# Feed-forward layers: the row panel of step i-1 moved from behind the up panel of step i to between the gate and the up panel

## The chip, the cores and the metric

The program runs on one core of a Trainium2 chip, as one launch. The metric is the time that the device takes for it, in microseconds. Five engines work side by side, each with its own queue in order: TensorE (PE, with its weight loads shown as PEld), VectorE (DVE), ScalarE (ACT), GpSimd (POOL) and SyncE (SP), which issues the transfers. They wait for each other by semaphores.

## What is computed

The reference is a stack of two blocks over 256 tokens of width 1024, in float32. The change touches only the feed-forward layers of the first block. There are four: `ffn1` and `ffn2` in each of two layers, each with a residual sum of one half.

```python
def swiglu(h, w_gate, w_up, w_down):
    return (jax.nn.silu(h @ w_gate) * (h @ w_up)) @ w_down
...
x = x + 0.5 * swiglu(rmsnorm(x, norm_ffn1[layer]), ffn1_gate[layer], ffn1_up[layer], ...)
```

`w_gate` and `w_up` are 1024 x 2816, `w_down` is 2816 x 1024. Around them stand the mixers (a linear recurrence, a gated delta rule, a gated recurrence) and a second block (retention, dilated attention, a feed-forward part with a squared relu, a gate), which the change leaves as they are.

## The kernel before, in words

**Precision.** Each float32 product is made of three products of a shorter format. A weight panel lands in `raw` (three slots, 1 MB each). ScalarE rounds it to `w_hi` (`split_hi`, L1470), VectorE subtracts to get `w_lo` (`split_lo`, L1947); both have two slots. The activation is split the same way: `u_both` holds the high and low halves of the normed input. An operand for the down product is split to `op_hi` (ScalarE, L1698) and `op_lo` (VectorE, L2015), in four slots.

**Panels.** A panel is one megabyte of weights. A feed-forward layer has 2816 / 256 = 11 steps, numbered 0 to 10. Step i has a **gate panel** and an **up panel** (column panels: all 1024 rows of 256 columns, result in the PSUM banks `colb`), and the down product has a **row panel** for each step: 256 rows of all 1024 columns, added up over the steps in the PSUM tile `acc`. From step 2 on a column panel writes two banks: the high weights meet both halves of the input in one matmul of 512 columns, 16 of them, and then the low weights meet the high half, 16 of 256 columns. A row panel has three thirds in this order: `w_hi` with `op_hi`, `w_lo` with `op_hi`, `w_hi` with `op_lo` (`row_part`, which waits for `w_lo_ready` ahead of the second third and for `op_ready` ahead of the last). The last row panel of a layer waits for all of it at its start.

**Behind a column panel.** ScalarE copies the second bank (`copy_half`, L1515), VectorE adds the first (`add_halves`, L1961). Behind a gate panel ScalarE then takes the silu (L1555). Behind an up panel VectorE multiplies the two into `hid` (L1995), which is the operand of this step: `op_hi` is made from it, and then `op_lo`.

**What sets the order.** `ffn` writes one list, `schedule`, of panels and steps. Every engine walks through the same list and does its part of each entry. With panel p, ScalarE first splits `w_hi` as far as panel p+1 (`split_hi_to`), and VectorE `w_lo` as far as panel p+1 (`split_lo_to`), before they turn to what panel p left in its banks. `split_hi` of panel p waits until TensorE is done with panel p-2, since there are two slots. SP issues the transfer of panel p when both halves of panel p-3 are made. So an entry that changes its place in the list changes it in every queue.

**Other entries.** In layer 0 of `ffn1`, small tables for the mixer are made on VectorE and ScalarE in steps 3 and 4, behind the gate panel (`setup`, `setup_rest`). Row panels 0 to 8 (`by_token`) are summed with tokens in the rows of `acc`. Behind row panel 8 `acc_out` copies `acc` out, and ahead of row panel 9 `acc_turn` (L1062) brings it back transposed with 16 matmuls. Step 0 and the first gate panel work on an input that isn't normed yet.

Of the kernel before, what the change touches and what calls it, by code (L numbers as in the profile page):

```python
# [23 lines left out]
KD = D // P  # L24
DEPTH = 2
D_FF = 2816
PC = 256
# [87 lines left out]
def build(nc, ap, out, stop_at=None):  # L115
    ctx = ExitStack()
    with ctx:
        def sb(name, shape, dt=F32):
            return ctx.enter_context(nc.sbuf_tensor(name, shape, dt))
# [20 lines left out]
        hid = sb("hid", [P, 2, 2 * T])  # L140
# [131 lines left out]
        schedule, panels, ops = [], [], []  # L272
# [8 lines left out]
        def panel(src, kt, ncols, kind, xop, ready, **more):  # L281
            nonlocal n_col, n_act, n_dve, n_row
            r = dict(p=len(panels), src=src, kt=kt, nc=ncols, kind=kind, xop=xop, ready=ready, **more)
            if kind != "row" and early[0]:
                n_scaled[0] += 1
                r.update(xop=g_op(early[1]["ops"]), ready=[], gained=count["fill"] if early[0] == EARLY else None, scaled=n_scaled[0],
                         norm=count["norm"], fill=early[1], half=EARLY - early[0])
                early[0] -= 1
                fresh[0] = True
            elif kind != "row":  # L290
                r["fresh"], fresh[0] = fresh[0], False
            if kind != "row":
                r["c"] = n_col
                n_col += 1
                if r["by"] == "act":
                    n_act += 1
                    r["n"] = n_act
                else:
                    n_dve += 1
                    r["n"] = n_dve  # L300
                bank_users.append((r["by"], r["n"]))
            else:
                n_row += 1
            panels.append(r)
            schedule.append(("panel", r))
            return r
# [33 lines left out]
        def step(name, **more):  # L340
            schedule.append((name, dict(panel=len(panels), nx=count["x"], op=len(ops), **more)))

        def g_op(n_ops):
            def get(kk):
                return tuple(gained_chunk(t, n_ops, kk // 2)[:, kk % 2, :] for t in (op_hi, op_lo))
            return get
# [16 lines left out]
        def pre_norm(gain, at):  # L363


            step("gained", gain=gain, at=at, n=count["fill"] + 1)
            n = norm_sum("x", "fill", gain=gain, at=at)
            f = fill(norm=n, gain=gain, at=at)
            return f

        def x_update(kind, **more):
            count["x"] += 1
            step("x_update", kind=kind, group=count["group"], first=0, **more)
            if kind in ("half", "whole"):
                acc_reader[0] = ("x_updated", 4 * count["x"])
            if kind == "post":
                count["normed"] += 1
                acc_reader[0] = ("acc_normed", 4 * count["normed"])

        def operand(src, ready):  # L380

            r = dict(r=len(ops), src=src, ready=ready)
            ops.append(r)
            return r
# [7 lines left out]
        def kpn(w):  # L392
            return w.rearrange("(k p) n -> p k n", p=P)

        def row_gemm_panel(w, i, r, first, last, base=None, woven=False, by_token=False):
            if r is not None:
                ready = [("op_ready", r["r"] + 1)]
                r["panel"] = len(panels)
                get = op_tiles(r)
            else:  # L400
                ready = base[0]
                get = (lambda kk, i=i: base[1](2 * i + kk))
            if first and acc_reader[0]:
                ready = ready + [acc_reader[0]]
            p = panel(kpn(w)[:, 2 * i:2 * i + 2, :], 2, D, "row", get, ready, first=first, last=last, woven=woven, by_token=by_token)
            if last:
                count["group"] += 1
            return p

        def acc_out():  # L410
            count["turn"] += 1
            step("acc_out", n=count["turn"])
# [3 lines left out]
        def two_banks(r, c0, pair):  # L416


            a = 0 if (c0 % 3 == 0) == (pair == 0) else 2
            r.update(both=n_both[0], banks=slice(a, a + 2),  # L420
                     free=[n for n in range(c0 - 3, c0) if n % 3 in (a, a + 1)] if r["c"] - c0 < 2 else None)
            n_both[0] += 1
            last_both[r["c"]] = n_both[0]

        def ffn(layer, gain, gate, up, down):
            f = pre_norm(gain, KD * layer)
            n = D_FF // PC
            todo = None
            first_both = None
            for i in range(n):  # L430
                g = panel(kpn(gate)[:, :, i * PC:(i + 1) * PC], KD, PC, "A", u_op, [("u_ready", 4 * f)],
                          by="act", evac=("silu_h", len(ops)))
                if i == 2:
                    first_both = g["c"]
                if i >= 2:
                    two_banks(g, first_both, 0)
                if (layer, i, gain) == (0, 3, "norm_ffn1"):
                    step("setup")
                if (layer, i, gain) == (0, 4, "norm_ffn1"):
                    step("setup_rest")  # L440
                if i:
                    step("op_lo", r=todo)
                u = panel(kpn(up)[:, :, i * PC:(i + 1) * PC], KD, PC, "A", u_op, [], by="dve",
                          evac=("h", len(ops), g["n"]))
                if i >= 2:
                    two_banks(u, first_both, 1)
                r = operand(hid[:, len(ops) % 2, :], [("dve_evac", u["n"])])
                if i:
                    if i == n - 1:
                        step("acc_turn", n=count["turn"])  # L450
                    row_gemm_panel(down, i - 1, todo, i == 1, False, by_token=i < n - 1)
                    if i == n - 2:
                        acc_out()
                step("op_hi", r=r)
                todo = r
            step("op_lo", r=todo)
            row_gemm_panel(down, n - 1, todo, n == 1, True)
            x_update("half")
# [87 lines left out]
        for l in range(DEPTH):  # L546
            ffn(l, "norm_ffn1", ap["ffn1_gate"][l], ap["ffn1_up"][l], ap["ffn1_down"][l])
            if stop_at == "ffn1":
                break
            mixer(l)  # L550
            if stop_at == "mix":
                break
            ffn(l, "norm_ffn2", ap["ffn2_gate"][l], ap["ffn2_up"][l], ap["ffn2_down"][l])
            if stop_at == "layer":
                break
# [2031 lines left out]
```

How the kernel before makes its waits and increments, by code:

```python
        def evacuated(eng, n):  # L733
            by, done = bank_users[n]
            eng.wait_ge(sem(f"{by}_evac"), done)
# [1 line left out]
        def col_bank_free(eng, n):  # L737
            evacuated(eng, n)
            both = [last_both[i] for i in (n, n + 1, n + 2) if i in last_both]
            if both:
                eng.wait_ge(sem("both_added"), both[-1])
# [1 line left out]
        def bank_done(eng, r, b):  # L744
            if b < 3:
                eng.wait_ge(sem("acc_bank"), 3 * (r["group"] - 1) + b + 1)
            else:
                eng.wait_ge(sem("panel_used"), r["panel"])
# [31 lines left out]
        @block.sync  # L781
# [7 lines left out]
                    p = r["p"]  # L789
                    if p == RAW_SLOTS:
                        sp.dma_start(cst[:, :], ap["constants"]).then_inc(sem("cst_loaded"), 16)
                        sp.dma_start(rg_w[:, :], ap["rg_w"]).then_inc(sem("rg_w_loaded"), 16)
                    if p >= RAW_SLOTS:
                        sp.wait_ge(sem("w_hi_ready"), p - RAW_SLOTS + 1)
                        sp.wait_ge(sem("w_lo_ready"), p - RAW_SLOTS + 1)
                    dst = raw[:, p % RAW_SLOTS, 0:r["kt"] * r["nc"]].rearrange("p (k n) -> p k n", k=r["kt"])
                    sp.dma_start(dst, r["src"]).then_inc(sem(f"raw_loaded{p % RAW_SLOTS}"), 16)
            for b in range(4):
                sp.wait_ge(sem("x_updated"), 4 * (n_x - 1) + b + 1)
                sp.dma_start(out[:, 2 * b:2 * b + 2, :], x[:, 2 * b:2 * b + 2, :]).then_inc(sem("stored"), 16)
            sp.wait_ge(sem("stored"), 64)
```

## Time and profile before

| | |
|---|---|
| timed runs, median (lowest to highest of 3) | 1785.44 us (1783.36 to 1785.57) |
| profiled execution, its own time | 1782.4 us |
| its span | 1780.6 us |
| TensorE busy | 1728.7 us, 97% of the span |
| VectorE busy | 1134.5 us, 64% |
| ScalarE busy | 971.1 us, 55% |
| GpSimd busy | 102.5 us, 6% |
| read from HBM | 287.81 MB, 162 GB/s over the span |
| mean granted clock of TensorE | 0.996 of full speed |

The profile is of one execution. Its page gives busy time by engine, the waits and what ended them, and the costliest groups of instructions; the trace behind it can be asked for a timeline of any stretch. TensorE's matmuls are pipelined, so the distance from one weight load to the next tells more of its pace than the length of one matmul.

### The profile page before, as it was taken

To read this page: it belongs to the slowest core of one execution; us is meant where nothing else is said; L and a number is where in the kernel's file an instruction comes from. 1 tells how busy PE (TensorE), PEld (TensorE's weight loads), DVE (VectorE), ACT (ScalarE), POOL (GpSimd) and SP (SyncE) were. 2 spreads that over 40 slices of the span, in tenths; PEclk is the share of its full clock that TensorE was granted. 3 is DMA by queue.
4 is the path that set the end of the run, shared out by engine and by line. 5 is a ranking of instruction groups with operands and counts; after the bars stand their busy time and mean duration, and the time that the engine had idled before them with its cause. 6 is when DMAs were issued, how large, how long until landed. Compare 5 with 4: busy or idle time off the path is not lost.

```text
span 1780.6 us, 30124 instructions
## 1 busy us (share of the span) xinstructions
PE 1728.7 (97%) x12956; PEld 1573.0 (88%) x12956; DVE 1134.5 (64%) x1338; ACT 971.1 (55%) x1105; POOL 102.5 (6%) x82
## 2 busy tenths in 40 slices
PE   8999999999999999999899999999999999999996
PEld 7878998898889888998898888989898879899996
DVE  5565788675557555698775556564465566775557
ACT  6544687564446444677664446543445464654445
POOL 0000001000000000001000000692000000000000
PEclk9999999999999999999999999999999999999999
DMA  7555562256555556563146564556255514455551
GB/s 260 184 184 181 168 190 73 73 163 193 189 189 166 191 188 198 168 190 96 50 148 200 181 204 152 183 190 204 94 166 189 166 66 165 159 181 190 189 173 41
DMA packets 206948, 290.80 MB, mean 163 GB/s; under 512 B 4608, under 2 KB 170624, under 8 KB 206688
## 3 DMA queue, kind: packets, MB, share of 16 engines
q1 hardware_dynamic: 206368, 287.11, 49.6%
q8 instruction: 102, 1.67, 0.4%
q0 software_dynamic: 448, 1.77, 0.3%
q14 instruction: 30, 0.25, 0.0%
HBM read 287.81 MB, written 1.05 MB: 162 GB/s over the span
## 4 chain that ended last, share of the span: by engine, by line
PE 81%; ACT 8%; DVE 6%; issue 2%; POOL 2%; DMA 0%; SPq 0%; DVEq 0%; ACTq 0%; POOLq 0%
PE colb L884 52%; PE acc L884 27%; ACT w_hi L1470 3%; DVE u L2043 2%; DVE w_lo L1947 1%; PE acc L1062 0%; DVE x L2079 0%; POOL arena L774 0%; DVE u L2078 0%; PE colb L1402 0%; ACT arena L1907 0%; ACT L1585 0%; ACT L1573 0%; ACT op_hi L1608 0%; ACT rstd L1589 0%
## 5 line engine op out<-in xcount | busy, mean ns | idle before, releaser
L1947 DVE TENSOR_TENSOR w_lo<-raw,w_hi 128x2048 fp32r<-128x2048 f32 x271 | 630.3, 2327 | 395.6 <-ACT w_hi L1470 395.0
L1470 ACT ACTIVATE w_hi<-raw 128x2048 fp32r<-128x2048 f32 x271 | 515.7, 1903 | 230.3 <-PE acc L884 179.0
L884 PE MATMUL colb<-u_both,w_hi 128*128 128x256 f32 (+1 forms) x3328 | 551.6, 321 | 0.9 <-ACT u_both L1681 0.2
L884 PEld LDWEIGHTS colb<-u_both,w_hi 128*128 128x128 f32 x3328 | 481.9, 190 | 49.1 <-ACT u_both L1681 3.5
L884 PE MATMUL colb<-u_both,w_lo 128*128 128x256 f32 x2240 | 291.2, 283 | 0.0
L884 PEld LDWEIGHTS colb<-u_both,w_lo 128*128 128x128 f32 x2240 | 283.2, 192 | 5.6
L884 PE MATMUL colb<-w_hi,u_both 128*128 128x512 f32 (+1 forms) x480 | 110.0, 378 | 0.3 <-ACT w_hi L1470 0.3
L884 PEld LDWEIGHTS colb<-w_hi,u_both 128*128 128x128 f32 x480 | 85.2, 188 | 16.8 <-ACT w_hi L1470 0.5
L884 PE MATMUL acc<-w_lo,op_hi 128*128 128x512 f32 x384 | 95.2, 390 | 3.2 <-DVE w_lo L1947 3.2
L884 PE MATMUL acc<-op_hi,w_hi 128*128 128x256 f32 x544 | 96.9, 286 | 0.9 <-ACT arena L1816 0.9
L884 PE MATMUL acc<-w_hi,op_hi 128*128 128x512 f32 x384 | 96.3, 392 | 0.4 <-ACT w_hi L1470 0.4
L884 PE MATMUL acc<-op_hi,w_lo 128*128 128x256 f32 x544 | 95.6, 284 | 0.2
L884 PE MATMUL acc<-op_lo,w_hi 128*128 128x256 f32 x544 | 95.0, 283 | 0.0
L884 PE MATMUL acc<-w_hi,op_lo 128*128 128x512 f32 x384 | 94.9, 389 | 0.0
L884 PEld LDWEIGHTS acc<-w_lo,op_hi 128*128 128x128 f32 x384 | 71.9, 188 | 19.2 <-DVE w_lo L1947 4.4
L1515 ACT ACTIVATE act_t<-colb 128x512 f32<-128x512 f32 x36 | 21.5, 598 | 122.6 <-PE colb L884 122.6
L884 PEld LDWEIGHTS acc<-w_hi,op_lo 128*128 128x128 f32 x384 | 72.1, 188 | 15.0
L884 PEld LDWEIGHTS acc<-w_hi,op_hi 128*128 128x128 f32 x384 | 69.0, 189 | 12.9 <-ACT w_hi L1470 0.6
L884 PEld LDWEIGHTS acc<-op_hi,w_hi 128*128 128x128 f32 x544 | 78.6, 191 | 1.5 <-ACT arena L1816 1.2
L884 PEld LDWEIGHTS acc<-op_hi,w_lo 128*128 128x128 f32 x544 | 78.5, 192 | 0.6 <-DVE w_lo L1947 0.6
L884 PEld LDWEIGHTS acc<-op_lo,w_hi 128*128 128x128 f32 x544 | 78.5, 192 | 0.0
L884 PE MATMUL acc<-arena 64*64 64x64 f32 (+3 forms) x1448 | 67.2, 232 | 9.1 <-ACT small L1772 6.2
(319 smaller groups left out, 1812.8 us busy)
## 6 DMA issues: line engine op xcount, KB each, us to landing
raw<-w_in SPq DMA_DIRECT2D x78, 1024.0 KB, 5.2
raw<-ffn_gate SPq DMA_DIRECT2D x44, 1024.0 KB, 5.3
raw<-ffn_up SPq DMA_DIRECT2D x44, 1024.0 KB, 5.3
raw<-ffn_down SPq DMA_DIRECT2D x44, 1024.0 KB, 4.9
raw<-w_up SPq DMA_DIRECT2D x16, 1024.0 KB, 5.4
raw<-w_down SPq DMA_DIRECT2D x16, 1024.0 KB, 4.9
raw<-w_out SPq DMA_DIRECT2D x8, 1024.0 KB, 5.3
raw<-w_ret_out SPq DMA_DIRECT2D x8, 1024.0 KB, 4.9
```

What stands on the lines that cost most here:

```text
L884: return pe.matmul(o, a, b, start=start, stop=stop, skip_group_check=True)
L1470: act.activation(split_view(w_hi, r), raw[:, p % RAW_SLOTS, 0:r["kt"] * r["nc"]], ACT.Copy)\
L1515: act.activation(both_dst(r).rearrange("p (m t) -> p m t", t=T), colb4[:, r["banks"], T:2 * T], ACT.Copy)\
L1947: tt(split_view(w_lo, r), raw[:, p % RAW_SLOTS, 0:r["kt"] * r["nc"]], split_view(w_hi, r).bitcast(F32), ALU.subtract).then_inc(sem("w_lo_r ...
L2043: ins = stt(u32[:, kk, :], x[:, kk, :], c(r["gain"], r["at"] + kk), rstd[:, :], ALU.mult, ALU.mult)
```

## The change

In each step i from 1 on the row panel of step i-1 is entered in the list right behind the gate panel of step i (and behind `op_lo`, which makes the low half of its operand), instead of behind the up panel of step i. `acc_turn` and `acc_out` go with it. Behind the loop the last row panel follows as before. No operation is added or removed.

```diff
                 if i:
                     step("op_lo", r=todo)
-                u = panel(kpn(up)[:, :, i * PC:(i + 1) * PC], KD, PC, "A", u_op, [], by="dve",
-                          evac=("h", len(ops), g["n"]))
-                if i >= 2:
-                    two_banks(u, first_both, 1)
-                r = operand(hid[:, len(ops) % 2, :], [("dve_evac", u["n"])])
                 if i:
                     if i == n - 1:
                         step("acc_turn", n=count["turn"])
                     row_gemm_panel(down, i - 1, todo, i == 1, False, by_token=i < n - 1)
                     if i == n - 2:
                         acc_out()
+                u = panel(kpn(up)[:, :, i * PC:(i + 1) * PC], KD, PC, "A", u_op, [], by="dve",
+                          evac=("h", len(ops), g["n"]))
+                if i >= 2:
+                    two_banks(u, first_both, 1)
+                r = operand(hid[:, len(ops) % 2, :], [("dve_evac", u["n"])])
                 step("op_hi", r=r)
                 todo = r
```

The order of the instructions shows it in three places. First ScalarE in a steady step of the first feed-forward layer, before:

```order
L1555 ACTIVATE act_t<-act_t 128x512
L1470 ACTIVATE w_hi<-raw 128x2048
L1515 ACTIVATE hid<-colb 128x512
L1470 ACTIVATE w_hi<-raw 128x2048
L1698 ACTIVATE op_hi<-hid 128x512
L1470 ACTIVATE w_hi<-raw 128x2048
L1515 ACTIVATE act_t<-colb 128x512
```

and of the changed kernel, in the same step:

```order
L1555 ACTIVATE act_t<-act_t 128x512
L1470 ACTIVATE w_hi<-raw 128x2048 x2
L1515 ACTIVATE hid<-colb 128x512
L1698 ACTIVATE op_hi<-hid 128x512
L1470 ACTIVATE w_hi<-raw 128x2048
L1515 ACTIVATE act_t<-colb 128x512
```

Of the three splits of a step, two now stand between the silu and the copy behind the up panel, and the one of the row panel's weights stands behind `op_hi`.

VectorE in step 4 of the first layer, where `setup_rest` ends (its last row here is L2150), before:

```order
L2150 TENSOR_SCALAR small<-small 128x4
L2015 TENSOR_TENSOR op_lo<-hid,op_hi 128x512
L1947 TENSOR_TENSOR w_lo<-raw,w_hi 128x2048
L1961 TENSOR_TENSOR hid<-colb,hid 128x512
L1995 TENSOR_TENSOR hid<-act_t,hid 128x512
L1947 TENSOR_TENSOR w_lo<-raw,w_hi 128x2048 x2
```

and of the changed kernel:

```order
L2150 TENSOR_SCALAR small<-small 128x4
L2015 TENSOR_TENSOR op_lo<-hid,op_hi 128x512
L1947 TENSOR_TENSOR w_lo<-raw,w_hi 128x2048 x2
L1961 TENSOR_TENSOR hid<-colb,hid 128x512
L1995 TENSOR_TENSOR hid<-act_t,hid 128x512
L1947 TENSOR_TENSOR w_lo<-raw,w_hi 128x2048
```

The first `w_lo` behind the tables was that of the row panel; in the changed kernel two splits stand there, of the up panel and the next gate panel, and the row panel's stands ahead of the tables.

TensorE at the end of a feed-forward layer (the rows of 128x256 without a count are the last row panel):

```order
 L884 MATMUL acc<-op_hi,w_lo 128x256 x16
 L884 MATMUL acc<-op_lo,w_hi 128x256 x16
+L884 MATMUL colb<-u_both,w_hi 128x512 x16
+L884 MATMUL colb<-u_both,w_lo 128x256 x16
 L884 MATMUL acc<-op_hi,w_hi 128x256
 L884 MATMUL acc<-op_lo,w_hi 128x256
```

The last up panel now stands between row panel 9 and row panel 10, which were neighbours before.

## Rows read from the trace of the kernel before

**Rows 1.** The page, busy time by engine: us, share, instructions.

```profile
PE 1728.7 (97%) x12956; PEld 1573.0 (88%) x12956; DVE 1134.5 (64%) x1338; ACT 971.1 (55%) x1105; POOL 102.5 (6%) x82
```

**Rows 2.** Waits of TensorE: who waited for what: us in total, times, longest.

```profile
PE acc L884 <- DVE w_lo L1947: 3.2, 3, 2.8
```

**Rows 3.** A stretch's busy times; timeline of a steady step: start, us, instructions [idle before].

```profile
113.33:129.91 16.58, 16.58 (x90) 14.35 (x89) 9.55 (x7) 7.87 (x7) 0.00 (x0) 1.00 0.57 191
...
118.98 3.51 PEld L884 LDWEIGHTS colb<-u_both,w_hi 128*128 128x128 f32 x16
...
124.55 1.70 PEld L884 LDWEIGHTS acc<-w_hi,op_hi 128*128 128x128 f32 x8
...
124.86 0.60 ACT L1515 ACTIVATE hid<-colb 128x512 f32<-128x512 f32 x1 [1.71 <-PE colb L884]
...
125.56 0.69 DVE L1961 TENSOR_TENSOR hid<-colb,hid 128x512 f32<-128x512 f32 x1
126.28 1.77 PEld L884 LDWEIGHTS acc<-w_lo,op_hi 128*128 128x128 f32 x8
126.36 0.69 DVE L1995 TENSOR_TENSOR hid<-act_t,hid 128x512 f32<-128x512 f32 x1
...
128.09 1.77 PEld L884 LDWEIGHTS acc<-w_hi,op_lo 128*128 128x128 f32 x8
```

**Rows 4.** Timeline of step 10, first layer: a rounding and a split behind it.

```profile
181.02 0.63 ACT L1698 ACTIVATE op_hi<-hid 128x512 fp32r<-128x512 f32 x1
181.54 1.92 ACT L1470 ACTIVATE w_hi<-raw 128x2048 fp32r<-128x2048 f32 x1
...
183.49 2.29 DVE L1947 TENSOR_TENSOR w_lo<-raw,w_hi 128x2048 fp32r<-128x2048 f32 x1 [2.15 <-ACT w_hi L1470]
```

**Rows 5.** Timeline of steps 3 and 4, first layer, with the setup tables.

```profile
59.40 3.59 PEld L884 LDWEIGHTS colb<-u_both,w_hi 128*128 128x128 f32 x16
...
77.13 3.59 PEld L884 LDWEIGHTS colb<-u_both,w_hi 128*128 128x128 f32 x16
...
83.72 0.69 DVE L1961 TENSOR_TENSOR act_t<-colb,act_t 128x512 f32<-128x512 f32 x1 [1.87 <-ACT act_t L1515]
...
90.26 0.69 DVE L2015 TENSOR_TENSOR op_lo<-hid,op_hi 128x512 fp32r<-128x512 f32 x1
90.87 2.28 DVE L1947 TENSOR_TENSOR w_lo<-raw,w_hi 128x2048 fp32r<-128x2048 f32 x1
...
93.21 1.68 PEld L884 LDWEIGHTS acc<-w_lo,op_hi 128*128 128x128 f32 x8 [3.17 <-DVE w_lo L1947]
...
96.76 3.59 PEld L884 LDWEIGHTS colb<-u_both,w_hi 128*128 128x128 f32 x16
```

**Rows 6.** The page, transfers: KB each, us from issue to landing.

```profile
raw<-ffn_up SPq DMA_DIRECT2D x44, 1024.0 KB, 5.3
```

**Rows 7.** Timeline of the first layer's end: row panel 9 and the load behind it.

```profile
196.41 1.99 PEld L884 LDWEIGHTS acc<-op_lo,w_hi 128*128 128x128 f32 x16
...
198.33 0.19 PEld L884 LDWEIGHTS acc<-op_hi,w_hi 128*128 128x128 f32 x1
```

**Rows 8.** Timeline of step 1, second layer of four: the first operand.

```profile
388.04 5.83 PEld L884 LDWEIGHTS colb<-u_both,w_hi 128*128 128x128 f32 x48
...
391.38 0.63 ACT L1698 ACTIVATE op_hi<-hid 128x512 fp32r<-128x512 f32 x1 [2.06 <-DVE hid L1995]
...
392.04 0.69 DVE L2015 TENSOR_TENSOR op_lo<-hid,op_hi 128x512 fp32r<-128x512 f32 x1 [0.70 <-ACT op_hi L1698]
```

**Rows 9.** A long wait; three stretches: length, busy PE, PEld, DVE, ACT, POOL; clock.

```profile
283.02 5.47 PE L884 MATMUL acc<-arena 128*128 128x128 f32 x32 [3.08 <-ACT small L1772]
...
280.00:290.00 10.00, 6.98 (x47) 6.98 (x47) 9.40 (x20) 5.59 (x9) 4.94 (x5) 0.83 0.22 91
820.00:830.00 10.00, 6.92 (x47) 6.72 (x46) 9.49 (x20) 5.55 (x10) 6.00 (x5) 0.83 0.33 106
93.00:97.00 4.00, 3.79 (x17) 3.12 (x18) 3.65 (x4) 0.63 (x1) 0.00 (x0) 1.00 0.67 217
```

## The prediction

> **What bounds the kernel now.** I read the page first: TensorE is busy in 97% of the span [rows 1]. The table of waits comes next: TensorE waits 52 us in all (1780.6 - 1728.7), and of the feed-forward layers only one entry stands high, the low halves of a weight panel, 3.2 us in three waits [rows 2]. Then the timeline of a steady step: it lasts 16.58 us, and TensorE is busy in every microsecond of it [rows 3]. A change that only reorders such a step can't make it shorter; it can only uncover waits. So the question is what each panel needs and how long that takes once the order is different. There are four feed-forward layers of eleven steps (0 to 10).
>
> **What the change does to the deadlines.** Before, the operand that step i-1 makes is used by the row panel behind the gate and the up panel of step i: it has two column panels of time. Afterwards it has one, in the last step none, and in step 1 less than it needs. The number of matmuls, transfers and splits is the same; the three queues that feed TensorE (SP, ScalarE, VectorE) only take the row panel's weights before the up panel's. POOL has nothing there. I go through the four places, with the chain measured from the load of the first weights behind the up panel (call it 0).
>
> *The chain.* The copy of the second bank starts at 0.31 (124.86 against 124.55) and lasts 0.60; the addition starts 0.03 later, the product starts 0.80 after the addition (125.56, 126.36) and lasts 0.69 [rows 3]. That gives copy 0.31, addition 0.94, product 1.74 to 2.43. The rounding op_hi can then start at 2.47. From its start ScalarE begins the next w_hi 0.52 later, and VectorE its w_lo 1.95 after that, which lasts 2.29 [rows 4].
>
> *Inside a layer (steps 3 to 9, 28 steps).* ScalarE now does copy, op_hi, w_hi of the row panel in a row: w_hi from 2.99, w_lo from 4.94 to 7.23. TensorE wants these low halves after the gate panel and the first third of the row panel: a column panel behind a column panel takes 5.57 (118.98 to 124.55), the third 1.73 (124.55 to 126.28) [rows 3], so at 7.30. The margin is 0.07 us less some 0.06 from the end of w_lo to the load, as at 93.15 and 93.21 [rows 5]: nothing to spare. The other deadlines have more: w_hi of the row panel is there at 4.9 for 5.57; op_lo, behind w_lo and the gate's addition, ends near 8.5 for 9.11 (the second third takes 1.81); w_hi of the up panel, behind that addition and the silu, ends near 10.4 for 10.9. I take 0 for these 28 steps; the bounds are 0 and 0.2 us each (5.6 in all), since starts in the steady rows agree within some hundredths. Below nothing it can't go, as TensorE has no idle time there. A stall of each step doesn't add up along the layer: the chain starts again at each up panel. The raw transfers go past each other in SP's queue too; each is issued when the low halves of the panel three before are done, over 8 us before its split wants it, against 5.3 us from issue to landing [rows 6].
>
> *The last row panel (step 10, four times).* Before, row panel 9 stood between the last up panel and row panel 10, which starts with no gap (196.41 plus 1.92 is 198.33) [rows 7]. Now row panel 10 follows its own up panel. It waits for both halves of its operand: product to 2.43, op_hi 2.47 to 3.10, op_lo 3.13 to 3.81 (0.69 [rows 8]), load at 3.87. Nothing covers this; its weights are ready. 4 x 3.87 = **15.5 us**.
>
> *The first row panel (step 1, four times).* The gate panel ends a third of the way through the 48 loads (three groups of 16) that start at 388.04, at 388.04 + 1.92 = 389.96. Row panel 0 wants op_hi, which ends at 392.01 [rows 8], so its load is at 392.04: 2.08 late. That time doesn't change, since the product behind it (DVE) waits for things that the change leaves where they are; op_lo is there at 392.73, when a third has run. 4 x 2.08 = **8.3 us**. Before, an up panel covered it.
>
> *Setup in layer 0, once.* In step 4 VectorE's small tables stand between the gate's addition (83.72) and op_lo (90.26), 6.54 us, of which 5.93 are the tables, since op_lo starts 0.61 behind an addition otherwise. Before, this delayed the row weights' low halves by 3.2 us and the step took 96.76 - 77.13 = 19.63 instead of 16.58 [rows 5]: 3.05 lost. Now the low halves come first and op_lo, 5.93 later, ends near 14.4 where 9.1 is wanted: 5.3 lost, net **+2.2 us**. In step 3 (17.73 us before, 1.15 lost [rows 5]) the tables are shorter; ScalarE's part stands ahead of w_hi of the up panel, whose margin is 0.5. I take the same loss, within 1 us.
>
> The waits add up to 15.5 + 8.3 + 2.2 = **26.0 us**.
>
> **The clock.** Behind a wait of 3.08 us the granted clock in 280 to 290 us is 0.83 on average, which is 0.17 x 10 = 1.7 us of full-speed work lost; the same wait in the other layer gave 0.83 as well. It fell from 2.4 to 1.2 GHz for part of the stretch. Behind the wait of 2.75 us at 93 us it stayed 1.00 [rows 9]. The changed kernel has five waits longer than both, the four last row panels and setup. So between 0 and 5 x 1.7 = 8.5 us come on top. The one that kept its clock is nearly as long as the two that lost it, so length alone doesn't settle it, and part of the low stretch can fall on the wait itself; I take three of five, **5.1 us**. The Trainium skill (TensorE: Matmul & The Clock Gate, section "HAM oscillation — how this bites in real kernels") states that waits of this kind between bursts return the array to its low clock and that the price is paid anew at each. By that rule all five fall and the sum would be 34.5 us.
>
> **Sum.** 26.0 + 5.1 = 31.1 us. The profiled execution took 1782.4 us (span 1780.6 and 1.8 around it), so 1813.5. The median of the three timed runs lies 3.0 above it, which gives 1816.5 on that scale; I take 1815.
>
> **The rivals.**
>
> *No clock falls.* The waits come as summed, and the clock holds as at 93 us: 1808.4, or 1811.4 on the median's scale.
>
> *All clocks fall and the steady steps are late too.* 26.0 + 8.5 = 34.5, and 0.2 in each of 28 steps 5.6 more: 1782.4 + 40.1 = 1822.5, or 1825.5. For it speaks the margin of nothing at 7.30; against it that TensorE starts its loads slightly ahead of its matmuls, so that a few hundredths are hidden.
>
> *Nothing to measure.* TensorE's order might not be what sets the end of a layer: if the step behind (residual sum, norm, next gate) were waited for anyway, a later row panel 10 would be hidden. But the timeline has TensorE going on from row panel 10 into the next column panels with no gap, so only a few of the 26 us could go; 1782 to 1786.
>
> *Faster.* In setup VectorE's low halves of the row weights now come ahead of the tables. If the operand were ready by then, the 3.05 and the 1.15 us of the two setup steps would be saved: 1778.2. It decides from the point at which the operand chain is shorter than the panels that stand between: 3.87 us is shorter than 5.57 in a steady step, but in the last step nothing stands between, and in setup op_lo is itself behind the tables. The order printed shows both.
>
> That the change isn't carried out is excluded by the same order: TensorE has an up panel between the last two row panels now.
>
> **How the numbers follow.** Forecast (waits as summed, some clocks fall) 0.50; no clock falls 0.15; all fall and late steps 0.23; a still larger loss, with a wait that I didn't see, 0.05; nothing to measure 0.04; faster 0.03. The range reaches from just below the case without clock falls, 1807, to the upper case, 1825. About 0.2%, 3.6 us, is what a measurement of this kernel can tell from no change. Slower 0.93, same 0.04, faster 0.03.
>
> **What would show it.** In the profile after: at the end of each feed-forward layer a load with an idle time near 3.9 us, released by op_lo; in step 1 one near 2.1 us, released by op_hi; one near 5.3 us in step 4 of the first layer, released by op_lo; steady steps still of 16.6 us; the granted clock below 1 behind the long ones. I am wrong if steady steps take 17 us or more (then the row weights' chain is late each time), or if the last row panel starts without a gap.

## The result

The changed kernel takes 1826.97 us (median of 4 runs, 1826.21 to 1827.43), the kernel before 1784.78 us (1783.36 to 1785.57): a ratio of 1.0237, 95% interval 1.0225 to 1.0249. It is 42.2 us slower. Forecast were 30 (1815 us), with a range up to 1825, so the direction was right and the size was outside the range.

The page of the changed kernel: its span, and busy time by engine (us, share, instructions), against [rows 1]:

```profile
span 1824.4 us, 30124 instructions
...
PE 1746.3 (96%) x12956; PEld 1586.3 (87%) x12956; DVE 1132.5 (62%) x1338; ACT 976.2 (54%) x1105; POOL 102.5 (6%) x82
```

The instructions are the same in number. TensorE waits 78.1 us (span less busy time) instead of 51.9, 26.2 more, and it is also *busy* 17.6 us longer for the same matmuls; together that is the 43.8 us between the two spans. The waits are new and named (in total, times, longest):

```profile
PE acc L884 <- DVE op_lo L2015: 20.0, 5, 5.0
PE acc L884 <- ACT op_hi L1698: 7.7, 4, 1.9
```

Five waits for `op_lo`: the four last row panels, and the last third of row panel 3 in step 4 of the first layer. Four for `op_hi`: row panel 0 of each layer. The row weights' low halves, the entry of [rows 2], are nearly gone. The end of the first layer, against [rows 7] (start, us, instruction, idle time before it):

```profile
207.15 0.69 DVE L1995 TENSOR_TENSOR hid<-act_t,hid 128x512 f32<-128x512 f32 x1
207.88 0.63 ACT L1698 ACTIVATE op_hi<-hid 128x512 fp32r<-128x512 f32 x1 [1.62 <-DVE hid L1995]
...
208.54 0.69 DVE L2015 TENSOR_TENSOR op_lo<-hid,op_hi 128x512 fp32r<-128x512 f32 x1 [0.70 <-ACT op_hi L1698]
209.35 0.29 PEld L884 LDWEIGHTS acc<-op_hi,w_hi 128*128 128x128 f32 x1 [3.93 <-issue]
209.38 0.55 PE L884 MATMUL acc<-op_hi,w_hi 128*128 128x256 f32 x1 [3.76 <-DVE op_lo L2015]
```

The chain product, `op_hi`, `op_lo`, load stands bare, with 3.93 us of idle loads. And the matmul behind it lasts 0.55 us, where the one of the kernel before lasted 0.28. Step 1 of the second layer, against [rows 8]:

```profile
404.58 0.63 ACT L1698 ACTIVATE op_hi<-hid 128x512 fp32r<-128x512 f32 x1 [2.06 <-DVE hid L1995]
...
405.32 2.91 PEld L884 LDWEIGHTS acc<-w_hi,op_hi 128*128 128x128 f32 x8 [2.10 <-issue]
405.35 3.60 PE L884 MATMUL acc<-w_hi,op_hi 128*128 128x512 f32 x8 [1.92 <-ACT op_hi L1698]
```

Eight loads take 2.91 us there; in a steady step they take 1.70 [rows 3]. What the two places have in common is the clock. Some stretches (length, busy PE, PEld, DVE, ACT, POOL, granted clock, DMA share, GB/s), against [rows 9]:

```profile
90.00:100.00 10.00, 5.45 (x17) 4.35 (x18) 6.03 (x23) 3.62 (x2) 0.00 (x0) 0.83 0.38 129
200.00:210.00 10.00, 6.24 (x36) 5.42 (x35) 4.37 (x4) 4.63 (x4) 0.00 (x0) 0.88 0.72 210
210.00:220.00 10.00, 10.00 (x69) 10.00 (x69) 6.58 (x10) 5.16 (x11) 0.00 (x0) 0.78 0.22 56
400.00:410.00 10.00, 8.08 (x43) 6.93 (x42) 7.53 (x7) 5.41 (x6) 0.00 (x0) 0.83 0.31 105
570.00:580.00 10.00, 6.46 (x32) 6.49 (x33) 5.56 (x6) 4.28 (x6) 0.00 (x0) 0.66 0.31 103
1130.00:1140.00 10.00, 6.24 (x39) 5.95 (x38) 4.15 (x5) 4.42 (x4) 0.00 (x0) 0.83 0.43 140
110.00:190.00 80.00, 80.00 (x420) 68.80 (x419) 47.06 (x37) 38.67 (x37) 0.00 (x0) 1.00 0.60 192
```

The clock went from 2.4 to 1.2 GHz for a part of each stretch around a wait: behind setup (90), at the first layer's end (200 and 210 together), behind the wait of 2.1 us at 400, and so on. Between them, over 80 us of steady steps, it is 1.00 and TensorE is never idle. The steady step is what was summed: the row weights' low halves end at 160.75 and their load starts at 160.80; from the same load of the step before it is 16.63 us, against 16.58 [rows 3].

```profile
144.17 1.76 PEld L884 LDWEIGHTS acc<-w_lo,op_hi 128*128 128x128 f32 x8
...
158.46 2.29 DVE L1947 TENSOR_TENSOR w_lo<-raw,w_hi 128x2048 fp32r<-128x2048 f32 x1 [2.50 <-ACT w_hi L1470]
...
160.80 1.31 PEld L884 LDWEIGHTS acc<-w_lo,op_hi 128*128 128x128 f32 x6
```

### The profile page after: what moved, and what is told of

Its sections match the earlier page's. It is cut to its first block, busy times and chain, and to the rows that moved or that the text cites. A ratio compares the mean times of both kernels' runs of the same rounds, so it can differ in the third digit from the quotient of the medians.

```text
span 1824.4 us, 30124 instructions
## 1 busy us (share of the span) xinstructions
PE 1746.3 (96%) x12956; PEld 1586.3 (87%) x12956; DVE 1132.5 (62%) x1338; ACT 976.2 (54%) x1105; POOL 102.5 (6%) x82
## 4 chain that ended last, share of the span: by engine, by line
PE 79%; ACT 9%; DVE 8%; issue 3%; POOL 2%; DMA 0%; SPq 0%; DVEq 0%; ACTq 0%; POOLq 0%
PE colb L884 50%; PE acc L884 27%; ACT w_hi L1470 3%; DVE w_lo L1947 2%; DVE u L2043 2%; PE acc L1062 0%; DMA raw<-ffn_gate 0%; DVE hid L1995 0%; DVE x L2079 0%; POOL arena L774 0%; DVE u L2078 0%; DVE u_both L2048 0%; PE colb L1402 0%; ACT arena L1907 0%; ACT L1585 0%
## 5 line engine op out<-in xcount | busy, mean ns | idle before, releaser
L884 PE MATMUL acc<-op_hi,w_hi 128*128 128x256 f32 x544 | 101.6, 295 | 16.0 <-DVE op_lo L2015 15.0
L884 PE MATMUL acc<-w_hi,op_hi 128*128 128x512 f32 x384 | 100.8, 406 | 7.7 <-ACT op_hi L1698 7.7
L884 PE MATMUL acc<-op_hi,w_lo 128*128 128x256 f32 x544 | 99.4, 291 | 0.3
L884 PE MATMUL acc<-op_lo,w_hi 128*128 128x256 f32 x544 | 99.1, 290 | 0.0
L884 PEld LDWEIGHTS acc<-op_hi,w_hi 128*128 128x128 f32 x544 | 82.9, 199 | 17.2 <-issue 15.7
L1515 ACT ACTIVATE hid<-colb 128x512 f32<-128x512 f32 x36 | 21.5, 598 | 125.5 <-PE colb L884 125.5
L1698 ACT ACTIVATE op_hi<-hid 128x512 fp32r<-128x512 f32 x60 | 37.7, 629 | 87.1 <-DVE hid L1995 84.7
L884 PEld LDWEIGHTS acc<-op_hi,w_lo 128*128 128x128 f32 x544 | 82.5, 199 | 0.7 <-DVE w_lo L1947 0.7
L884 PEld LDWEIGHTS acc<-op_lo,w_hi 128*128 128x128 f32 x544 | 82.8, 200 | 0.0
```

Source lines behind the costliest of these rows:

```text
L884: return pe.matmul(o, a, b, start=start, stop=stop, skip_group_check=True)
L1515: act.activation(both_dst(r).rearrange("p (m t) -> p m t", t=T), colb4[:, r["banks"], T:2 * T], ACT.Copy)\
L1698: act.activation(op_hi[:, r["r"] % OP_SLOTS, :], src, ACT.Copy).then_inc(sem("op_hi_ready"), 1)
```

## The experiments

Theory A: the 42 us are the three exposed waits and a lower clock around them. Theory B: they are spread over all steps, by a chain that is late each time or a clock that is low throughout. Times are medians; intervals are of the ratio to the kernel before on the same chip.

### Undoing the change at one place

The row panel's place is chosen by step; its block stands once ahead of the up panel and once behind it. `early_row` is `i < n - 1` in the first of these runs (step 10 as before), `i > 1` in the second (step 1 as before), `2 <= i < n - 1` without setup's two steps in the third, and `i == n - 1` in the fourth.

```diff
+                early_row = i < n - 1
-                if i:
+                if i and early_row:
...
                 u = panel(
...
+                if i and not early_row:
...
```

**Step 10 as before, the rest new.** 

> The changed kernel with step 10 of each layer in the old order (row panel 9 behind the last up panel). Theory A (the change costs its three exposed waits plus a lower clock behind them): the layer ends cost 4 x 3.9 us of waiting and about 2.3 us of clock each, so this takes some 24 to 26 us off the changed kernel, to 1801 to 1803 us. Theory B (the waits are small change; the operand chain is late in every step, or the clock is low over the whole layer): only the share of one step in ten comes back, some 4 us, 1823 us.

Measured: 1802.70 us, ratio 1.0103 (1.0089 to 1.0117). That is 24.3 us below the changed kernel. The four ends make up more than half of the loss. Of it 15.7 us are waiting (4 x 3.93). The rest can be read off the stretch from the last row panel's first load to the first instruction of the next input's norm (L2043): 16.81 us before (198.33 to 215.14), 18.97 after (209.35 to 228.32), 2.16 more; in the other three layers, read in the same way, 2.63, 2.56 and 1.29 more. 15.7 + 8.6 is 24.3. That the two agree to a tenth is luck, since the runs of one kernel lie 1.2 to 1.5 us apart here.

**Step 1 as before, the rest new.** 

> The changed kernel with step 1 of each layer in the old order. Theory A: 4 x 2.1 us of waiting and about 1.5 us of clock in three of the four layers come back, 12 to 14 us off, 1813 to 1815 us, and the stretches behind the first row panel show a granted clock of 1.00. Theory B: 4 us off, 1823 us.

Measured: 1811.66 us, ratio 1.0153 (1.0139 to 1.0167), 15.3 us below the changed kernel, somewhat more than A's 12 to 14; its four runs spread over 4.1 us (1809.44 to 1813.55), and the excess isn't explained further. The `op_hi` waits are gone and the clock stays up in those stretches:

```profile
400.00:410.00 10.00, 10.00 (x70) 9.27 (x69) 6.88 (x6) 5.35 (x5) 0.00 (x0) 1.00 0.48 162
600.00:610.00 10.00, 10.00 (x53) 8.59 (x52) 4.96 (x3) 3.61 (x3) 0.00 (x0) 1.00 0.65 210
```

**Only the inner steps new.** 

> Only the inner steps in the new order: step 1, steps 3 and 4 of the first layer (setup) and step 10 are as before. Theory A: the 34 inner steps cost 0.0 to 0.07 us each, so 0 to 2 us above the kernel before, 1785 to 1787 us, with the same two clock falls as before, both in the mixers. Theory B: most of the 42 us is still there.

Measured: 1786.27 us, ratio 1.0009 (1.0001 to 1.0018): 1.7 us, by the interval 0.2 to 3.2, for 30 steps (eight in each layer, less the two of setup; the 34 of the expectation are a miscount). Theory B falls. One thing was not as expected: the clock fell a third time, in step 4 of the first layer, whose wait is the old one of 2.8 us for the row weights (this stretch reads 1.00 in the kernel before, [rows 9]):

```profile
90.00:100.00 10.00, 7.24 (x25) 5.43 (x25) 7.72 (x15) 3.03 (x3) 0.00 (x0) 0.83 0.40 112
```

So a wait of one and the same length kept its clock in one execution and lost it in another. A fall like this one may be part of the 1.7 us.

**Only step 10 new, on the kernel before.** 

> The kernel before with step 10 alone in the new order. If the parts add up, this costs what the first study of the last step gives back: 24 to 26 us above the kernel before, 1809 to 1811 us, with a wait of 3.8 us ahead of each last row panel. If the cost of the ends comes from the inner steps' order (queues that have shifted by then), it is far less.

Measured: 1808.96 us, ratio 1.0145 (1.0131 to 1.0159), 25.1 us above the kernel before. The parts add up; the ends need nothing from the other steps' order.

```profile
PE acc L891 <- DVE op_lo L2022: 15.0, 4, 3.8
```

### The clock apart from the waits

TensorE gets idle matmuls in the new waits: ones by ones into a bank whose contents have been read (`fill_wait` first waits until the banks of the panel named are read). There are 34 ahead of the last row panel in the first try, 17 in the second.

```diff
+            def fill_wait(q, n):
...
+                for _ in range(n):
+                    mm(o, ones, ones)
...
                 if r["kind"] == "row" and r["last"]:
                     pe.wait_ge(sem("w_lo_ready"), p + 1)
+                    if "both" in panels[p - 1] and "both" in panels[p - 3]:
+                        fill_wait(panels[p - 3], 34)
                     if op_ready:
                         pe.wait_ge(sem("op_ready"), op_ready)
...
                 elif r["kind"] == "row":
+                    if r["by_token"] and r["first"] and panels[p - 3].get("scaled"):
+                        fill_wait(panels[p - 3], 18)
                     if op_ready:
                         pe.wait_ge(sem("op_hi_ready"), op_ready)
```

The same ahead of row panel 0 (18, then 9; the last lines of the diff) and ahead of the last third of row panel 3 in the first layer (46, then 23). The condition for row panel 0 also holds once in a feed-forward layer of the second block, where TensorE had nothing to wait for. So there are ten groups of idle matmuls for nine waits. The tenth, in the second try, and the same load in the changed kernel, where it has no idle time before it:

```profile
1603.49 2.08 PEld L884 LDWEIGHTS colb<-one_row 128*128 128x128 f32 x18
1605.49 1.69 PEld L884 LDWEIGHTS acc<-w_hi,op_hi 128*128 128x128 f32 x8
...
1617.49 1.68 PEld L884 LDWEIGHTS acc<-w_hi,op_hi 128*128 128x128 f32 x8
```

Between two splits of weights around it (`w_lo`, 1597.58 to 1613.29 in the second try, 1611.58 to 1625.77 in the changed kernel) it costs 1.5 us, and in the first try, read in the same way, 3.5.

**First try.** 

> The changed kernel with idle matmuls (ones by ones, 128 columns, into a bank that nobody reads any more) on TensorE in the waits ahead of row panel 0 (18), the last row panel (34) and the last third of row panel 3 of the first layer (46). The waits stay as long as they are; only TensorE is busy in them. Theory A: the clock no longer falls there, and 13 to 16 us come back, 1811 to 1814 us; the granted clock's mean is 0.996 as before. Rival (the low clock has another cause, or costs nothing since the stretch waits for other engines anyway): 1827 us, or more by the added matmuls.

Measured: 1841.95 us, ratio 1.0330 (1.0314 to 1.0346), slower by 15 us than the changed kernel: not theory A's number, and above 1827 as the rival allowed for added matmuls. The timeline tells why: 34 of them show as 68 and last 7.68 us, in a wait of 3.93.

```profile
211.00 7.68 PEld L884 LDWEIGHTS colb<-one_row 128*128 128x128 f32 x68
```

They overran by some 28 us in all (2.0 and 3.8 us four times each, 5 us once), and the tenth group added 3.5. The kernel lost only 15 of these 31 to 32 us: the difference points to the clock, but as a time this run is inconclusive. It was repeated at half the number.

**Second try.** 

> The same as the filled kernel, with half the number of idle matmuls (9, 17 and 23). In the filled kernel each of them showed as two and lasted 0.226 us, so that they overran the waits (7.68 us in a wait of 3.9); 9, 17 and 23 take 2.0, 3.8 and 5.2 us, just less than the waits of 2.1, 3.9 and 5.4 us. Theory A: the clock stays up at all nine places and nothing else changes, 13 to 16 us less than the changed kernel, 1811 to 1814 us. Rival: the low clock costs nothing on the path, 1827 us.

Measured: 1814.33 us, ratio 1.0163 (1.0149 to 1.0176), 12.6 us below the changed kernel, a hair outside the 13 to 16 expected. The waits are as long as before, and the clock is up everywhere in the layers:

```profile
203.98 3.88 PEld L884 LDWEIGHTS colb<-one_row 128*128 128x128 f32 x34
...
200.00:210.00 10.00, 10.00 (x78) 9.54 (x77) 4.71 (x5) 3.74 (x4) 0.00 (x0) 1.00 0.65 204
210.00:220.00 10.00, 10.00 (x89) 9.78 (x92) 9.85 (x14) 8.10 (x14) 0.00 (x0) 1.00 0.21 56
570.00:580.00 10.00, 10.00 (x85) 10.00 (x85) 8.64 (x14) 7.07 (x13) 0.00 (x0) 1.00 0.32 107
```

The 12.6 us hold the tenth group as a loss of 1.5 us, so the clock is worth some 14.1. The two profiles, compared place by place, give 15.1: 8.7 us at the four ends (from the last row panel's first load to L2043), 4.8 us in step 1 of three layers and 1.6 us in setup. Step 1 of the second layer, from the first load of row panel 0 to that of row panel 1, takes 18.36 us in the changed kernel (405.32 to 423.68) and 16.79 here (402.77 to 419.56). What remains is 29.3 us above the kernel before on the same chip, the 1.5 of the tenth group among them.

### The margin of the inner steps

`op_hi` is made twice for the operands of steps 2 to 8, which lengthens the chain from the up panel and nothing else.

```diff
+                if r.get("again"):
+                    link(act.activation(op_hi[...], src, ACT.Copy))
                 act.activation(op_hi[...], src, ACT.Copy).then_inc(sem("op_hi_ready"), 1)
```

**On the kernel before.** 

> The kernel before with op_hi made twice, one after the other, for the operands of steps 2 to 8: some 0.7 us more on the chain from the up panel's end. In the old order two column panels cover it: no change, within 1 us of the kernel before.

Measured: 1784.40 us, ratio 1.0001 (0.9992 to 1.0010).

**On the changed kernel.** 

> The changed kernel with the same second op_hi. If the chain of the inner steps has no margin left, as summed before the run, each of the 28 steps 3 to 9 is 0.6 to 0.75 us longer: 17 to 21 us above the changed kernel, 1844 to 1848 us. If there is a margin that the sum missed (0.7 us or more), no change.

Measured: 1847.13 us, ratio 1.0352 (1.0338 to 1.0367), 20.2 us above the changed kernel, or 0.72 in each of 28 steps. In the timeline `op_hi` comes 0.66 apart, and the table of waits has the loads of the low halves waiting 31 times, 0.6 us each:

```profile
PEld acc L885 <- DVE w_lo L1950: 19.2, 31, 0.6
...
126.77 0.63 ACT L1700 ACTIVATE op_hi<-hid 128x512 fp32r<-128x512 f32 x1 [1.62 <-DVE hid L1998]
127.43 0.63 ACT L1701 ACTIVATE op_hi<-hid 128x512 fp32r<-128x512 f32 x1
...
132.24 1.69 PEld L885 LDWEIGHTS acc<-w_lo,op_hi 128*128 128x128 f32 x8 [0.64 <-DVE w_lo L1950]
```

The new order has no margin in the inner steps; the old one hides the same work altogether.

### Moving the tables

```diff
-                if (layer, i, gain) == (0, 3, "norm_ffn1"):
-                    step("setup")
-                if (layer, i, gain) == (0, 4, "norm_ffn1"):
-                    step("setup_rest")
...
                 step("op_hi", r=r)
+                if (layer, i, gain) == (0, 3, "norm_ffn1"):
+                    step("setup")
+                if (layer, i, gain) == (0, 4, "norm_ffn1"):
+                    step("setup_rest")
```

**On the changed kernel.** 

> The changed kernel with the mixer's tables at the end of steps 3 and 4, behind op_hi. Theory: the wait for op_lo behind the tables (5.4 us), its lower clock (1.5 us) and the 1.7 us of step 3 go: 8 to 9 us off the changed kernel, 1818 to 1819 us. If the tables then push the chain of step 5, whose margin is nothing, some of it stays: up to 1823 us.

Measured: 1824.60 us, ratio 1.0222 (1.0208 to 1.0236), only 2.4 us off and above even the cautious end. The wait didn't go, it changed its cause:

```profile
106.21 2.29 DVE L1947 TENSOR_TENSOR w_lo<-raw,w_hi 128x2048 fp32r<-128x2048 f32 x1
108.55 3.06 PEld L884 LDWEIGHTS acc<-w_lo,op_hi 128*128 128x128 f32 x8 [3.45 <-DVE w_lo L1947]
```

In the new order VectorE turns to the row weights right behind the product, so tables entered there stand ahead of them: 3.45 us of waiting, and eight loads of 3.06 us that show the low clock again.

**On the kernel before.** 

> The kernel before with the tables of the mixer (setup, setup_rest) entered at the end of steps 3 and 4, behind op_hi, where VectorE and ScalarE stand idle for 2.6 us, instead of behind the gate panel. Theory: the 1.15 and 3.05 us of waiting for weight halves in these steps go, 4 us off the kernel before, 1780 to 1781 us. Rival: the tables then delay the low halves of the next up panel, and the 3 us only move; no change.

Measured: 1780.34 us, ratio 0.9982 (0.9973 to 0.9991). It is faster than both kernels, by 3.5 us than the one before (0.2%, and the interval leaves out 1). The wait of 3.2 us is gone; one of 0.56 us is left in step 4:

```profile
89.77 1.68 PEld L884 LDWEIGHTS acc<-w_lo,op_hi 128*128 128x128 f32 x8 [0.56 <-DVE w_lo L1947]
```

**That, and the mixers' waits filled.** 

> The kernel before with the tables late, and 13 idle matmuls (2.9 us) on TensorE in the wait of 3.3 us that each of the two mixers has ahead of the scores of the gated delta rule. If waits bring the clock down whatever their place, and the clock costs on the path, both mixers keep 1.00 and 2 to 3.4 us more go: 1777 to 1778.5 us. If the mixer isn't bound by TensorE behind that wait, 1780 to 1781 us, as with the tables late alone.

Besides the late tables the edit is one line at the head of TensorE's part of `gd_scores`: `keep_warm(r["c"], 13)`, which issues 13 idle matmuls (the step is handed the panel's number for it). Measured: 1780.47 us, ratio 0.9973 (0.9963 to 0.9983). The interval overlaps that of the tables alone, and the spans of the two profiles are 1778.8 and 1778.4 us: no gain is clear of the noise. The clock did stay up, and the 32 matmuls behind the first mixer's wait took 3.65 us instead of 5.28:

```profile
280.00:290.00 10.00, 9.82 (x85) 9.49 (x84) 9.74 (x20) 6.90 (x9) 2.62 (x2) 1.00 0.01 2
820.00:830.00 10.00, 9.82 (x85) 9.63 (x84) 9.80 (x20) 6.59 (x9) 4.09 (x3) 1.00 0.14 54
...
280.43 3.65 PEld L884 LDWEIGHTS acc<-arena 128*128 128x128 f32 x32 [0.37 <-ACT small L1773]
```

VectorE is busy in 97 and 98% of these stretches. In the first mixer the low clock cost TensorE's time but not the kernel's: from one split of weights ahead of it to one behind it (`w_lo`) it is 114.51 us with the tables alone (238.46 to 352.97) and 114.47 with the wait filled (238.70 to 353.17).

The second mixer is no such test. With the tables alone its wait of 3.08 us kept its clock in the profiled execution, where the kernel before had 0.83 [rows 9]; the clock fell 40 us later, behind waits of 0.6 us and less. There it did cost time: 16 loads took 3.28 us instead of 1.98, and the stretch between the splits around it is 1.2 us longer than in the filled kernel.

```profile
820.00:830.00 10.00, 8.16 (x70) 8.16 (x71) 9.80 (x19) 6.80 (x9) 3.91 (x3) 1.00 0.12 48
860.00:870.00 10.00, 9.15 (x139) 8.51 (x134) 6.40 (x7) 5.89 (x12) 0.00 (x0) 0.83 0.22 71
...
864.49 3.28 PEld L884 LDWEIGHTS acc<-op_hi,w_hi 128*128 128x128 f32 x16 [0.60 <-ACT arena L1816]
```

## Why the prediction was right and wrong

**The steady state and the chain: right.** The margin was summed to nothing from rows 3 and 4; the inner steps cost 0.06 us each (0.01 to 0.11 by the interval), and 0.66 more on the chain cost 0.72 a step.

**The three waits: right.** Summed were 3.87, 2.08 and 5.3 us; measured are 3.93, 2.10 and 5.41 us (by the idle time of the loads). 4 x 3.93 + 4 x 2.10 + 2.2 (5.41 less the old wait of 3.17) is 26.3 us, where the sum had 26.0, and TensorE's waiting grew by 26.2. Step 3, taken as unchanged at 1.15 lost, lost 1.5 (18.12 us from the row panel's first load to the next, 67.50 to 85.62).

**The clock: wrong, and it is nearly the whole miss.** The step that failed reads: "The changed kernel has five waits longer than both, the four last row panels and setup. So between 0 and 5 x 1.7 = 8.5 us come on top", and then "I take three of five". That gave a term of 5.1 us. It measured 12.6 us as a difference of medians, 14.1 without the tenth group and 15.1 place by place in the traces, each above the upper bound of the term itself. Three things were mis-sized:

- *Which waits count.* The bound took only waits longer than those seen. But the waits of 2.1 us ahead of row panel 0 brought the clock down too, in three of the four layers of the changed kernel. The one wait of 2.75 us that kept its clock [rows 9] was used as a bound, with shorter ones left out as safe. It was a single case, and the same wait lost its clock in the run with only the inner steps new. So eight of nine new waits lost it, where five were counted as candidates.
- *How many of the long ones.* All five fell, not three. The Trainium skill's rule (TensorE: Matmul & The Clock Gate, section "HAM oscillation — how this bites in real kernels"), which the prediction cited and set aside, would have been the better forecast for these: the trace agrees with it at all five.
- *How much each costs.* The 1.7 us came from the mixers. At the ends of the first three layers it was 2.2 to 2.6 (at the fourth 1.3, in step 1 and setup 1.6): in 570 to 580 us the mean clock is 0.66, twice the loss of [rows 9], and a part of the low stretch lies on the wait itself.

The expectation of the mixers shows the other half of this error. The 1.7 us were a fair reading of what TensorE loses there (5.28 against 3.65 us), and still cost the first mixer's stretch nothing, where VectorE is the busy one. In the feed-forward layers TensorE is busy all the time, and each such microsecond is on the path.

**The sum, repaired.** 26.3 of waits, 14.1 to 15.1 of clock and 1.7 of the inner steps are 42.1 to 43.1 us. Measured are 42.2 between the medians and 43.8 between the spans of the two profiles. What is left is within what these runs can tell apart.

**The point and the range.** The sum came to 1816.5 us, and 1815 was taken without a reason; that added 1.5 us to the miss. The upper case (all five clocks, late inner steps) gave 1825.5 and was cut to 1825; it reached that far only through 5.6 us for late steps, which didn't come. A clock term with nine places would have gone to 1782.4 + 3.0 + 26.0 + 9 x 1.7 = 1826.7 without them, and past 1832 with them. That the first of these lies at the measured time is partly luck: eight places fell, not nine, and their prices were not all 1.7.

## What to carry to other kernels

Where an engine is busy all the time, count for every operand how much work stands between its last input and its first use, at the first and the last pass of the loop too: an order that holds in the middle can be bare at both ends, and here the ends and the start cost some 40 us, the middle 1.7. Price each new wait of TensorE as the wait plus a low clock behind it, also for waits of 2 us, and count a wait's clock as lost unless several executions show that it isn't. Then ask whether TensorE is what the stretch waits for; if not, the low clock may cost nothing. To tell the two apart, fill the wait with idle matmuls that are timed to end just before it does, and look in the trace for every place where they landed.

## What the runs showed of the hardware

- Waits of 2.1 us in otherwise full stretches were followed by 1.2 GHz in three of four layers; the same wait of 2.8 us kept 2.4 GHz in one execution and not in another, and so did the second mixer's wait of 3.08 us (0.83 in the kernel before, 1.00 with the tables late). Length alone doesn't tell.
- A float32 matmul of ones by ones, 128 x 128, shows as two records and takes 0.226 us (7.68 us for 34), so that 34 of them overran a wait of 3.93 us. Such matmuls do hold the clock up: 1.00 at all nine places in the second try.
- A low clock behind the first mixer's wait cost 1.63 us of TensorE's time (5.28 against 3.65 us for the same 32 matmuls) and none of the kernel's (114.51 against 114.47 us). One 40 us behind the second mixer's wait, with no wait over 0.6 us just ahead of it, cost 1.3 us of TensorE's time (3.28 against 1.98 us for the same 16 loads) and 1.2 of the kernel's.
